# The recurrent stage with tiles folded in pairs, its softplus later, and memory keys and values as direct fp32 products

## The reference

```
o_inter = einsum('blhk,bhkv->blhv', qc * exp(cum), s)
decay   = exp(where(tri, cum[:, :, None] - cum[:, None, :], -inf))
scores  = einsum('bthk,bshk,btshk->bths', qc, kc, decay)
o_intra = einsum('bths,bshv->bthv', scores, vc)
s_new   = exp(last)[..., None] * s + einsum('bshk,bshv->bhkv', kc * exp(last[:, None] - cum), vc)
```

## Time and profile before

| | us |
|---|---|
| median of three runs (1726.11 to 1729.11) | 1728.59 |
| the profiled execution | 1725.81 |
| its span | 1723.9 |
| PE busy | 1659.0 |
| DVE busy | 1180.2 |
| ACT busy | 805.4 |

### The profile page before, as it was taken

How to read it: one execution, slowest core, us unless ns; L and a number is a source line. 1 busy time by engine, 2 the same in 40 slices (tenths; PEclk the granted TensorE clock), 3 DMA queues, 4 the chain that set the end, 5 groups by cost and what they waited for, 6 DMA issues and landing times.

```text
span 1723.9 us, 26838 instructions
## 1 busy us (share of the span) xinstructions
PE 1659.0 (96%) x10590; PEld 1480.3 (86%) x10590; DVE 1180.2 (68%) x1745; ACT 805.4 (47%) x1277; POOL 34.6 (2%) x49
## 2 busy tenths in 40 slices
PE   9999999999999998999998989999999999999998
PEld 8877777888999988888987889999999978888886
DVE  6477877675858589655345696665666786767686
ACT  5587777763434356413255453333332433333344
POOL 1000000000000001100000000000000000000001
PEclk9999999999999999899999999999999999999999
DMA  5232121201102142440253223333333953434332
GB/s 193 77 86 76 53 79 50 79 25 39 38 27 65 43 163 76 172 174 27 74 137 96 88 72 141 141 141 141 141 141 134 332 194 126 156 134 159 122 98 110
DMA packets 157694, 190.50 MB, mean 111 GB/s; under 512 B 5505, under 2 KB 117761, under 8 KB 155522
## 3 DMA queue, kind: packets, MB, share of 16 engines
q1 hardware_dynamic: 157570, 188.79, 33.3%
HBM read 134.58 MB, written 54.20 MB: 110 GB/s over the span
## 4 chain that ended last, share of the span: by engine, by line
PE 44%; DVE 4%; ACT 2%; issue 2%; DMA 1%; POOL 0%; DVEq 0%; ACTq 0%; POOLq 0%; SPq 0%
PE PS L2760 6%; PE PS L2762 6%; PE PS L2761 6%; PE PS L2581 6%; PE PS L2577 6%; PE PS L2579 6%; PE PS L1925 1%; PE PS L1924 1%; PE PS L1923 1%; PE PS L583 1%; DVE sbuf_gg_X L2849 1%; PE PS L2459 1%; PE PS L2461 1%; PE PS L2460 1%; PE PS L2025 0%
## 5 line engine op out<-in xcount | busy, mean ns | idle before, releaser
L621 PE MATMUL PS<-sbuf_h_hi,sbuf_w_hi 128*128 128x384 f32 x600 | 211.9, 353 | 6.0 <-ACT sbuf_g_N L632 2.7
L623 PE MATMUL PS<-sbuf_h_hi,sbuf_w_lo 128*128 128x384 f32 x600 | 201.8, 336 | 0.0
L622 PE MATMUL PS<-sbuf_h_lo,sbuf_w_hi 128*128 128x384 f32 x600 | 201.7, 336 | 0.0
L2760 PE MATMUL PS<-sbuf_ops_w,sbuf_go_u 128*128 128x512 f32 x448 | 175.2, 391 | 3.3 <-DVE sbuf_gg_X L2849 3.3
L2761 PE MATMUL PS<-sbuf_ops_w,sbuf_go_u 128*128 128x512 f32 x448 | 174.4, 389 | 0.0
L2762 PE MATMUL PS<-sbuf_ops_w,sbuf_go_u 128*128 128x512 f32 x448 | 174.3, 389 | 0.0
L2577 PE MATMUL PS<-sbuf_ops_S,sbuf_ops_w 128*128 128x288 f32 x512 | 150.9, 295 | 3.3 <-DVE sbuf_ops_S L2438 1.3
L2581 PE MATMUL PS<-sbuf_ops_S,sbuf_ops_w 128*128 128x288 f32 x512 | 151.1, 295 | 0.0
L2579 PE MATMUL PS<-sbuf_ops_S,sbuf_ops_w 128*128 128x288 f32 x512 | 150.7, 294 | 0.0
L621 PEld LDWEIGHTS PS<-sbuf_h_hi,sbuf_w_hi 128*128 128x128 f32 x600 | 113.3, 189 | 16.2 <-issue 10.0
L2602 ACT ACTIVATE sbuf_ff_u<-PS 128x576 f32<-128x576 f32 x64 | 41.6, 649 | 172.0 <-DMA uD<-sbuf_ff_sums 100.2
(11 more groups left out here) (324 smaller groups left out, 3920.0 us busy)
## 6 DMA issues: line engine op xcount, KB each, us to landing
sbuf_gg_u<-uD SPq DMA_DIRECT2D x28, 1024.0 KB, 5.2
uD<-sbuf_ff_u SPq DMA_DIRECT2D x16, 1152.0 KB, 4.2
sbuf_ff_raw<-w_ffn SPq DMA_DIRECT2D x16, 1024.0 KB, 6.2
sbuf_gg_B<-w_ffn SPq DMA_DIRECT2D x16, 1024.0 KB, 8.1
sbuf_raw<-w_in SPq DMA_DIRECT2D x28, 512.0 KB, 4.8
uD<-sbuf_ff_sums SPq DMA_DIRECT2D x16, 768.0 KB, 6.2
sbuf_X<-x_prompt SPq DMA_DIRECT2D x16, 512.0 KB, 7.3
xD<-sbuf_X SPq DMA_DIRECT2D x9, 512.0 KB, 2.6
```

What stands on the lines that cost most here:

```text
L621: pe.matmul(out, hi, h_hi[:, kb, tok], start=kb == 0, stop=False)
L622: pe.matmul(out, hi, h_lo[:, kb, tok], start=False, stop=False)
L623: last = pe.matmul(out, lo, h_hi[:, kb, tok], start=False, stop=kb == KB - 1)
L2760: pe.matmul(out, u_hi, x_hi, start=first, stop=False, skip_group_check=True)
```

## The change

1. **Pairs.** The odd tiles of the prompt are kept in reversed order of time: values (g_N[2], copied by copy_group with turned), and keys (g_kT). In factors, the even tiles fill the halves as before, and each odd tile, reversed, fills the halves that held leftovers, so that one product serves a pair. The slots are four pairs, and tile 8 as a fifth at levels 1 to 4. DVE's factors become four instructions for two. The levels are picked into g_S (pick), and a new step, spread, copies them from there to g_A, three masked copies a head. Level 0 keeps nine products and three picks (diagonals). The masks grow from 8 to 11.
2. **Softplus later.** The exponential of g_E goes behind the copy and cut of level 6, its logarithm behind those of level 7.
3. **Memory.** mem_kv is eight products of plain fp32 for each unit instead of 24. ACT copies the weights in two halves (mem_weights), DVE's cuts of these eight units and its four h_lo go.
4. g_S is set to zero at the start of the stage; the masks land in s_cV instead of c_q.

```diff
@@ hg_pe, mem_kv
-                    hi, lo = w_hi[s][:, kb * P:(kb + 1) * P], w_lo[s][:, kb * P:(kb + 1) * P]
-                    pe.matmul(out, hi, mem_h(h_hi, kb), start=kb == 0, stop=False)
-                    pe.matmul(out, hi, mem_h(h_lo, kb), start=False, stop=False)
-                    last = pe.matmul(out, lo, mem_h(h_hi, kb), start=False, stop=kb == KB - 1)
+                    w = mem_w[s][:, kb * P:(kb + 1) * P]
+                    last = pe.matmul(out, w, mem_h(r_hi, kb), start=kb == 0, stop=kb == KB - 1)
@@ hg_pe, levels
+                for n in range(1, NLV + 1):
+                    fill()
...
+                    pe.wait_ge(G["ql"], h * NLV + n)
+                    if n > 1:
+                        pe.wait_ge(G["pred"], h * NPK + 1 + n)
+                    for j in range(slots(n)):
+                        if n == 1 and j == 4:
+                            pe.wait_ge(G["pred"], h * NPK + 3)
+                        cols = slice(j * P, (j + 1) * P)
+                        last = pe.matmul(level_out(n)[:, j, :], g_KL[:, cols], g_QL[:, cols], start=True, stop=True)
@@ hg_pe, outputs
                 pe.wait_ge(G["qe"], h + 1)
+                pe.wait_ge(G["pred"], h * NPK + NPK)
@@ hg_act
-                step(g_kT[:], g_F[:], ACT.Exp, "k")
+                act.activation(tiles_in(g_kT)[:, 1:SMP:2, :], tiles_in(g_F)[:, 1:SMP:2, ::-1], ACT.Exp)
+                step(tiles_in(g_kT)[:, 0:NT:2, :], tiles_in(g_F)[:, 0:NT:2, :], ACT.Exp, "k")
...
+            def mem_weights(act, c, s):
+                k, n = unit(c, s)
+                act.wait_ge(landed[s % 2], n * 16 + 16)
+                act.wait_ge(slot_free[s], k + 1)
+                w = mem_w[s]
+                act.activation(w[:, 0:512], raw[s % 2][:, 0:512], ACT.Copy).then_inc(cut_hi[s % 2], 1)
+                act.activation(w[:, 512:1024], raw[s % 2][:, 512:1024], ACT.Copy).then_inc(cut_lo[s % 2], 1)
...
+                    if n == 6:
+                        act.wait_ge(G["gcap"], h + 1)
+                        step(g_E[:], g_E[:], ACT.Exp, "gln", scale=-1.0)
+                    if n == 7:
+                        act.wait_ge(G["gln"], h * 2 + 1)
+                        step(g_E[:], g_E[:], ACT.Ln, "gln", bias=1.0)
@@ hg_dve
+            od.then(dve.memset(g_S[:], 0.0))
...
+                dve.tensor_tensor(ql[:, :, :, 1, :], q[:, :, :, 1, :], d[:, :, :, 1, :], ALU.mult)
+                dve.tensor_tensor(kl[:, :, :, 0, :], k[:, :, :, 0, :], d[:, :, :, 0, :], ALU.mult)
+                d, q = (split(tiles_in(x)[:, 1:SMP:2, ::-1]) for x in (g_D, query_of(h)))
+                k = split(tiles_in(g_kT)[:, 1:SMP:2, :])
+                dve.tensor_tensor(ql[:, 0:4, :, 0, :], q[:, :, :, 0, :], d[:, :, :, 0, :], ALU.mult)
+                dve.tensor_tensor(kl[:, 0:4, :, 1, :], k[:, :, :, 1, :], d[:, :, :, 1, :], ALU.mult)\
                    .then_inc(G["ql"], 1)
...
+            def pick(h, n):
+                dve.wait_ge(G["lvl"], h * NL + 3 + n)
+                if n > 1:
+                    dve.wait_ge(G["pred"], h * NPK + 2 + n)
+                masked(g_S[:, 0:slots(n), :], n, level_out(n))
+
+            def spread(h):
+                dve.wait_ge(G["pred"], h * NPK + NPK - 1)
+                for tiles, mask, x in ((slice(0, SMP, 2), MASK_UP, g_S[:, 0:4, :]),
+                                       (slice(1, SMP, 2), MASK_BACK, g_S[:, 0:4, ::-1]),
+                                       (slice(SMP, NT), MASK_16, g_S[:, 4:5, :])):
+                    out = g_A[:, tiles, :]
+                    ins = dve.copy_predicated(out, lvl[:, mask, :].unsqueeze(1).broadcast_to([P, out.shape[1], P]), x)
+                ins.then_inc(G["pred"], 1)
```

More of the change, by code:

```diff
@@ L60 @@
 RAWS = 2
+MASK_ODD, MASK_UP, MASK_BACK, MASK_16 = (len(LEVELS) + 1 + i for i in range(4))
+MASKS = MASK_16 + 1
 C_ID, C_TRI, C_NEG, C_TRI16, C_NEG16, C_BLK, C_STR, C_ONE = 0, 128, 256, 384, 400, 416, 672, 680
@@ L271, in build @@
         g_ur, u_ring = [gg["u0"], gg["u1"]], [go[f"u{i}"] for i in range(RING)]
+        mem_w = list(layout("mem", F32, *((A_WHI + i * 1024, f"w{i}", (1024,)) for i in range(SLOTS))).values())
         landed = [sem(f"landed{i}") for i in range(RAWS)]
@@ L1050, in build @@
         G = {n: sem("hg_" + n) for n in names}
-        lchunks = []
-        for n in range(len(LEVELS) + 1):
-            tiles = NT if n == 0 or LEVELS[n - 1] < NQ else SMP
-            lchunks += [(n, t, min(4, tiles - t)) for t in range(0, tiles, 4)]
-        NL = len(lchunks)
         NLV = len(LEVELS)
+        NL = 3 + NLV
+        NPK = 3 + NLV + 1
         LASTH = HG_HEADS - 1
@@ L1060, in lcols, with tiles_in, slots, level_bank @@
             return T if n == 0 or LEVELS[n - 1] < NQ else SEQ
-        def last_chunk(n):
-            return max(c for c, x in enumerate(lchunks) if x[0] == n)
+        def tiles_in(x):
+            return x[:].rearrange("p (t c) -> p t c", c=P)
+        def slots(n):
+            return 5 if LEVELS[n - 1] < NQ else 4
+        def level_bank(n):
+            return 2 * (n % 2)
+        def level_out(n):
+            b = level_bank(n)
+            return PS[:, b:b + 2, :].rearrange("p a c -> p (a c)")[:, 0:slots(n) * P]\
+                .rearrange("p (s c) -> p s c", c=P)
         HG_ORDER = (1, 2, 3, 0)
@@ L1093, in hg_cuts @@
             c, s = {2: (h + 1, 3), 5: (h + 1, 0), 6: (h + 2, 1), 7: (h + 2, 2)}.get(n, (None, None))
-            return [(unit(c, s), s)] if c is not None and h < LASTH else []
+            return [(c, s)] if c is not None and h < LASTH else []
         M = {n: sem("mem_" + n) for n in
-             "in gain sq ms rs xn tr hi lo ev kt kte rows hr lr sq1 sqa ss rows2 st mean pow".split()}
+             "in gain sq ms rs xn tr hi ev kt kte rows hr lr sq1 sqa ss rows2 st mean pow".split()}
         KV = [(R_MEM + j // 4, j % 4) for j in range(8)]
@@ new lines, in hg_pe @@
+                if h == LASTH:
+                    pe.wait_ge(G["i"], h * 3 + 3)
+                    pe.wait_ge(G["sout"], h)
+                pe.matmul(PS[:, 3, 0:P], g_kT[:, SEQ:T], query_of(h)[:, SEQ:T], start=True, stop=True)\
+                  .then_inc(G["lvl"], 1)
+                for n in range(1, NLV + 1):
+                    fill()
+                    if h == LASTH:
+                        last_fill(n)
+                    if h and n == 2:
+                        hg_means(pe, h - 1, 4)
+                    pe.wait_ge(G["ql"], h * NLV + n)
[6 more added lines that the diff above has]
+                        last = pe.matmul(level_out(n)[:, j, :], g_KL[:, cols], g_QL[:, cols], start=True, stop=True)
@@ L1545, in factors, with split @@
                 dve.wait_ge(G["dexp"], h * NLV + n)
+                m = LEVELS[n - 1]
+                def split(x):
+                    return x.rearrange("p t (b h m) -> p t b h m", h=2, m=m)
                 if n > 1:
-                    dve.wait_ge(G["lvl"], h * NL + last_chunk(n - 1) + 1)
-                d, q, k = (halves(x[:], n) for x in (g_D, query_of(h), g_kT))
+                    dve.wait_ge(G["lvl"], h * NL + n + 2)
                 if n == 1:
@@ L1554, in factors @@
                         dve.wait_ge(G["o"], 2 * h)
[L1555 to L1570 removed]
+                ns = slots(n)
@@ new lines, in factors, with masked, diagonals @@
+                dve.tensor_tensor(ql[:, 0:4, :, 0, :], q[:, :, :, 0, :], d[:, :, :, 0, :], ALU.mult)
+                dve.tensor_tensor(kl[:, 0:4, :, 1, :], k[:, :, :, 1, :], d[:, :, :, 1, :], ALU.mult)\
+                   .then_inc(G["ql"], 1)
+            def masked(out, mask, x):
+                shape = out.shape
+                dve.copy_predicated(out, lvl[:, mask, :].unsqueeze(1).broadcast_to([P, shape[1], P]), x)\
+                   .then_inc(G["pred"], 1)
+            def diagonals(h):
+                for c, (tiles, mask, b) in enumerate(((slice(0, SMP, 2), 0, 0), (slice(1, SMP, 2), MASK_ODD, 1),
+                                                      (slice(SMP, NT), 0, 3))):
+                    dve.wait_ge(G["lvl"], h * NL + c + 1)
+                    out = g_A[:, tiles, :]
+                    masked(out, mask, PS[:, b, 0:out.shape[1] * P].rearrange("p (t c) -> p t c", c=P))
@@ L1636, in hg_dve @@
                 factors(h, 1)
-                pick(h, 0)
+                diagonals(h)
                 for n in range(1, NLV + 1):
@@ L1655, in hg_dve @@
                         forget_cap(h + 1)
-                    for use, s in hg_cuts(h, n):
-                        cut_lo_unit(dve, use, s)
+                    for c, s in hg_cuts(h, n):
+                        if c < R_MEM:
+                            cut_lo_unit(dve, unit(c, s), s)
                 if h < LASTH:
@@ L1662, in hg_dve @@
                 else:
+                    spread(h)
                     row_low(2)
```

122 lines of the change are left out of this document (50 added, 72 removed).

## The result

The changed kernel takes 1704.21 us (median of four runs, 1702.27 to 1706.05); the kernel before, beside it, 1727.35 (1724.56 to 1729.11). The ratio is 0.9867, with a 95% interval of 0.9848 to 0.9887. Measured once more at the end of the study, on another chip, it was 1706.89 against 1726.21, 0.9886 (0.9873 to 0.9900). The forecast was 1704.8. The profiled execution took 1705.12 with a span of 1703.2, 20.7 less than the span before.

What follows compares the result with a forecast made beforehand. PE was taken to bound the first three heads, DVE the fourth's first part, nobody throughout. Net 14.6 us plus the last head's 9.2 make 23.8; 1728.6 - 23.8 = 1704.8 us, range 1698 to 1714.

Steps and rivals of the forecast that it cites:

- Softplus later: First three heads, level 6: the 0.25 us a head by which the softplus steps had delayed it would go.
- Products of the levels: PE's levels: 28 fewer products save 5.97 us a head; period 6.20 becomes 5.34 us, 5.12 at levels 5 to 7.
- DVE would keep up with the period: Levels: DVE needs 2.5 us behind the last product, PE's fill takes 4.27, so 1.7 us to spare.
- Backwards operands: DVE's factors: reading tiles backwards costs nothing extra; at twice the time of an element, 0.53 us more a level.
- the slower rival: Backwards operands or strided masked copies take an expensive path; at 8 ns an element, 1760 us; chance 0.05.
- Behind level 7: PE's next fill waits 0.75 us more a head for ACT, losing nearly all of level 7's saving of 0.85.
- the late weights: In the first rival (1712.8 us, chance 0.21), raw weights come 0.3 to 1 us late for ACT's cut at level 7.
- The start: Start of the stage: DVE's new memset of 1024 elements and keys in two pieces lengthen PE's wait, 1.3 us lost.
- The last head: Fourth head: PE bound from level 3's end, level 4 at 663.2, first state at 700.8 for 709.97; gains 9.2 us.
- the clock rival: Last head: lower granted clock falls in the bound part, costing up to 8.8 of 9.2 us; 1713.6 us, chance 0.07.
- The lock: Last head: POOL's addition holds DVE's second subtraction to 690.1; without such a lock, 2.4 us earlier and a sum of 26.2.
- the memory part by itself: Last head: a memory unit costs PE 0.53 us more, eight of them 4.2; the gain is on DVE.

Runs made afterwards that it cites:

- The loaded DVE: Changed kernel with two memsets of 128 x 400 ahead of DVE's factors of levels 2 to 7 in the first three heads: 1708.16 us, ratio 0.9891.
- the two executions without the fall: Traced first heads of the changed kernel without its memory part (76.15 us) and with extra DVE memsets (76.18 us), where the clock stayed up.

## Why the prediction was right

**Products of the levels.** Forecast periods 5.34 and 5.12, measured 5.31 and 5.05. The loaded DVE shows that this is PE's gain. That DVE would keep up with the period held; I had 1.7 us of room, and the load proves about 1 us of it in most levels and 0.6 in levels 4 and 5 of the second and third heads.

**Backwards operands.** No extra cost, as taken: 0.42 us for 256 elements in either direction. From start to start it is 0.34, and 0.40 for 320 elements, as reckoned; I had named 0.40 or less as the length to look for, and 0.42 is within what the forward ones show too. The masked copies ran at the usual price, so the slower rival had nothing to stand on.

**Behind level 7.** I charged 0.75 us a head for a fill that would wait 1.3 us. It waits 1.00, 1.11 and 1.35, and with the logarithm moved 0.58: 0.4 to 0.8 a head, the right mechanism, a little dear.

**Softplus later.** I priced it at 0.25 us a head, reading how long level 6 was delayed before. Undone in the changed kernel it costs 5.7 us, 1.0, 2.5 and 2.7 in the first three heads. The sum did not suffer, for I had also taken level 6 to be on time; the value that I gave to this edit was wrong. I had raised the late weights only as a rival, at level 7; they show at level 5's cut, 0.51 us late in the changed kernel.

**The start.** The memset was to cost 1.3 us; PE's wait grew 0.8, and then the clock fell for 3.4 us, at a price near 1.5. The first head ended 1.9 us above what it would be without the memset by my other terms (81.24 - 5.4 = 75.84), where I had 1.3; in the two executions without the fall it ended 0.3 above. The mechanism of this step was incomplete: I reckoned a longer wait and not what stands behind it.

**The last head.** My times count from level 0 of this head, beside those of both executions of the changed kernel:

| | forecast | changed | again |
|---|---|---|---|
| level 3 | 14.7 | 14.92 | 14.50 |
| level 4 | 19.2 | 20.66 | 19.17 |
| level 7 | 42.7 | 44.39 | 42.87 |
| keys' transposes | 48.9 | 50.59 | 49.07 |
| first state | 56.8 | 58.35 | 56.84 |

The chain came out within 0.2 us in one execution, and 1.5 late in the other, where PE ran the norm's transposes and level 3 at 1.2 GHz (level 3's start is 0.4 later there, and level 4 another 1.1). That is the clock rival, at 1.5 us and not 8.8. The mean granted clock of the head is 0.90, so 2 x 0.10 x 65.42 = 13 us of it ran at 1.2 GHz, against 17.6 before; most of it lies where PE has waits to lose, and none in the bound part from level 4 to level 7.

**The lock.** The 3.85 us beside POOL came as forecast, and moving POOL's addition took 2.42 us out of the pair. The Trainium skill, "SBUF — State Buffer", section "SBUF: two separate sides", says that the two engines exclude each other for a whole instruction; this pair of runs agrees (3.85 with POOL at work, 1.43 without). What I said it was worth, 2.4 us of the sum, is some 0.8 us of the last head: POOL's addition holds up another DVE instruction by 0.64 us, and then PE is the next bound.

**The sum.** 23.8 us were forecast: 21.97 in the stage of the first execution, 23.5 in that of the second, 23.1 between the medians and 19.3 between the later ones. That 1704.21 met 1704.8 within 0.6 us is in part luck. I started from 1728.6, where the median of four runs is 1727.35. The first head's start came out 0.6 us worse than its term, the three fills behind level 7 together 0.5 better, the last head 1.3 worse or 0.2 better by the execution, and the stretch behind the stage, which I had put at nothing, 1.6 worse. By the later pair of medians the gain forecast is 4.5 us too large. What the sum also hides is how the last head's gain divides. By my working the memory part by itself loses on PE; the kernel with it alone is 4.3 us faster by the medians. Between single traces the last head gives it 6.5 to 6.9 us and the pairs 1.0 to 1.4, but each of these figures contains a difference in the clock of up to 3.8 us, so the shares of that head stay open.

## What to carry to other kernels

When a change shortens the bound engine's work in a loop, list what comes at fixed time (a transfer, another engine's long instruction) and see whether it now lands behind its use: here the old place of a softplus would have cost 5.7 of some 17 us. A wait of 2 to 3 us on TensorE can have a second price behind it, the work at 1.2 GHz (3.8 us behind one wait of 3.42 here), so short waits are often worth more than their length. Measure the parts of a two-part change one by one, for the total can be right while a share is wrong, and trace the same kernel twice before you read a difference of 1 or 2 us between single traces.
